# Sample keys turned in 32x32 blocks on VectorE and scored by 32-row matmuls, in a hybrid attention step on one Trainium2 core

## The reference

```python
z = rms_norm(x) @ w_in                        # q, k, v of branches A and B, gates
# A: 3 groups (window, dilation) = (128,1), (512,4), (2048,16), 8 heads of 64
idx = L + arange(t)[:, None] - arange(n + 1)[None, :] * dilation   # a query reads every d-th key
scores = einsum('bthd,btshd->bhts', q, k_ext[:, idx]) * d ** -0.5 - slope * steps * dilation
out_g = softmax(scores) @ v_ext[:, idx];  out_A = softmax(lse over groups) . out_g
# B: 4 heads, two maps over all 2048 + 8 keys (through page_table)
out_B = (softmax(q1 k1 - alibi) - lam * softmax(q2 k2 - alibi)) @ v
y = x + (sig(ma) * (silu(ga) * out_A @ w_a) + sig(mb) * (silu(gb) * rms(out_B) @ w_b)) @ w_out
```

## Time and profile before

| | us |
|---|---|
| median of 3 runs | 2002.45 (1999.88 to 2004.5) |
| the profiled execution | 2006.53 |
| its span | 2004.7 |
| TensorE busy | 1787.8 (89%) |
| VectorE, ScalarE, GpSimd busy | 623.6, 563.1, 620.6 |
| granted clock, mean | 0.953 |

### The profile page before, as it was taken

How to read it: one execution, slowest core, us unless ns; L and a number is a source line. 1 busy time by engine, 2 the same in 40 slices (tenths; PEclk the granted TensorE clock), 3 DMA queues, 4 the chain that set the end, 5 groups by cost and what they waited for, 6 DMA issues and landing times.

```text
span 2004.7 us, 31885 instructions
## 1 busy us (share of the span) xinstructions
PE 1787.8 (89%) x11560; PEld 1445.0 (72%) x11560; DVE 623.6 (31%) x1543; ACT 563.1 (28%) x1348; POOL 620.6 (31%) x763
## 2 busy tenths in 40 slices
PE   4899889999999999999957788777869999899899
PEld 3677556877799989999845565555647777677677
DVE  3321466221542217221533333333440104320321
ACT  3321356221442217220522222222211112211210
POOL 4663310466424644464500000000151215321210
PEclk8999999999999999999978889998889999899899
DMA  4136210434133441435169999999753754131542
GB/s 143 43 105 221 85 40 11 158 134 164 41 107 115 170 170 44 152 136 195 56 177 309 331 317 317 331 326 324 241 193 112 243 195 157 62 103 50 189 158 79
DMA packets 152794, 325.98 MB, mean 163 GB/s; under 512 B 24137, under 2 KB 45130, under 8 KB 151114
## 3 DMA queue, kind: packets, MB, share of 16 engines
q1 hardware_dynamic: 149130, 235.14, 36.1%
q10 hardware_dynamic: 3520, 88.90, 12.3%
HBM read 289.71 MB, written 121.57 MB: 205 GB/s over the span
## 4 chain that ended last, share of the span: by engine, by line
PE 68%; DMA 12%; issue 6%; POOL 5%; SPq 4%; DVE 3%; ACT 1%; ACTq 0%; DVEq 0%; POOLq 0%
PE ps L1573 15%; PE ps L1577 15%; PE ps L1574 15%; PE ps L1655 3%; PE ps L1606 3%; PE ps L1697 3%; PE ps L1675 3%; DMA v_in<-in_cache_a_kv 3%; DMA k_in<-in_cache_a_kv 2%; DMA raw<-in_w_in 2%; PE ps L1662 2%; DMA k_in<-in_cache_b_kv 2%; DMA v_in<-in_cache_b_kv 2%; POOL w_lo L719 1%; PE ps L1627 1%
## 5 line engine op out<-in xcount | busy, mean ns | idle before, releaser
L1573 PE MATMUL ps<-w_hi,hT_hi 128*128 128x512 f32 (+1 forms) x1440 | 591.1, 410 | 14.8 <-DVE w_lo L1137 6.5
L1577 PE MATMUL ps<-w_hi,hT_lo 128*128 128x512 f32 (+1 forms) x1440 | 579.3, 402 | 0.0
L1574 PE MATMUL ps<-w_lo,hT_hi 128*128 128x512 f32 (+1 forms) x1440 | 578.0, 401 | 0.0
L1573 PEld LDWEIGHTS ps<-w_hi,hT_hi 128*128 128x128 f32 (+1 forms) x1440 | 316.8, 220 | 71.8 <-issue 6.8
L1577 PEld LDWEIGHTS ps<-w_hi,hT_lo 128*128 128x128 f32 (+1 forms) x1440 | 316.5, 220 | 56.9 <-issue 0.4
L1574 PEld LDWEIGHTS ps<-w_lo,hT_hi 128*128 128x128 f32 (+1 forms) x1440 | 317.2, 220 | 53.5 <-issue 0.2
L719 POOL TENSOR_TENSOR w_lo<-raw,w_hi 128x512 fp32r<-128x512 f32 x160 | 210.0, 1315 | 433.6 <-ACT w_hi L884 433.3
L884 ACT ACTIVATE w_hi<-raw 128x512 fp32r<-128x512 f32 x176 | 110.3, 630 | 350.4 <-DMA raw<-in_w_in 302.9
L1697 PE MATMUL ps<-ident,k_in 128*128 128x128 f32 x928 | 140.0, 299 | 40.6 <-DMA k_in<-in_cache_b_kv 16.6
L1697 PEld LDWEIGHTS ps<-ident,k_in 128*128 128x128 f32 x928 | 112.3, 153 | 82.9 <-issue 44.0
L785 POOL TENSOR_SCALAR qz<-qT 64x128 f32<-64x128 f32 x208 | 109.2, 525 | 83.8 <-PE ps L1655 72.9
(11 more groups left out here) (159 smaller groups left out, 2063.3 us busy)
## 6 DMA issues: line engine op xcount, KB each, us to landing
out<-in_cache_a_kv ACTq DMA_DIRECT2D x32, 2040.0 KB, 8.4
raw<-in_w_in SPq DMA_DIRECT2D x144, 256.0 KB, 3.6
k_in<-in_cache_b_kv SPq DMA_DIRECT2D x128, 256.0 KB, 4.4
v_in<-in_cache_b_kv SPq DMA_DIRECT2D x128, 256.0 KB, 5.6
k_in<-in_cache_a_kv SPq DMA_DIRECT2D x104, 256.0 KB, 6.4
v_in<-in_cache_a_kv SPq DMA_DIRECT2D x104, 256.0 KB, 5.1
out<-in_cache_a_kv ACTq DMA_DIRECT2D x8, 2016.0 KB, 9.1
o_scr<-qT SPq DMA_DIRECT2D x16, 512.0 KB, 3.5
```

The source lines that it names most:

```text
L1573: pe.matmul(z, sh, w_hi[u % 2][:, k, :], start=(k == 0), stop=False)
L1574: pe.matmul(z, sh, w_lo[u % 2][:, k, :], start=False, stop=False)
L1577: ins = pe.matmul(z, sl, w_hi[u % 2][:, k, :], start=False, stop=(k == K - 1))
```

## The change

The key tiles are no longer turned by TensorE. VectorE transposes every 32x32 block of a tile in place, in `k_in`. After that, partitions 32i to 32i+31 hold, for each block of 32 keys, 32 of the head dimensions: a partition block i is a block of the tile's keys, and the columns `c * 128 + 32 * j` name the part j of the dimensions. A score is then a sum over four parts j, each a matmul over 32 rows; the four partition blocks i go to four PSUM banks and the four pairs c to four column blocks, so that a group of four tiles is 4 x 4 x 4 matmuls with 16 stationary columns and 128 streamed keys. GpSimd copies the queries to all four partition blocks (`q_rep`, rows now (c, half, query), 16 for each c).

The dilated tiles are scored against all eight queries; a table `bias_sa` holds 1e30 where a query does not read a key, as for the pages. So branch A's scores are 13 x 128 + 32 columns instead of 408. The groups are now 4, 4, 4, 1 tiles and four times four pages; key slots are 3 groups of four and are free once the group is scored; value slots are 12. Probabilities are transposed in nine pieces of up to four tiles through one bank (bank 4), copied by ScalarE to one of two buffers `pT`. The new keys and values are also stored in a DRAM scratch `new_scr` by sample and read back per sample. The minimum of branch B is taken over 4 partition-block strips with a table `ahead`, and its exponential is four instructions and one for the new keys.

```diff
+FIRST_S = (0, 4, 8, 12, 13, 17, 21, 25, 29)
+COLS_A = TILES_A * 32
+KEYS_A = TILES_A * P + NEW
...
-        NKS, NVS = 8, 16
+        NKS, NVS = 3, 12
+        k_in = place("k_in", [P, NKS, 4, CW], at=at)
...
+        def pieces_at(gg):
+            b, n = divmod(gg, 8)
+            if n >= 5:
+                return [(b, n - 5)]
+            return [(b - 1, p) for p in ((3,), (4,), (5,), (6,), (7, 8))[n]] if b else []
+        def keys_of(t, i, tiles):
+            return t[:, 0:tiles * P].rearrange("p (t f r) -> p t f r", f=4, r=32)[:, :, i, :]
...
-            for g in range(4):
-                sp.dma_start(v_in[0:NS, g, :], kept_new(g, 0)).then_inc(kn_in, 16)
...
-                    if kk >= NKS:
-                        sp.wait_ge(s_kt, kk - NKS + 1)
-                    sp.dma_start(k_in[:, kk % NKS, :], rows_s(kk, 0)).then_inc(sk_in[kk % NKS], 16)
+                    gg, j = key_slot(kk)
+                    b = kk // TILES_S
+                    if j == 0 and gg >= NKS:
+                        sp.wait_ge(s_qk, gg - NKS + 1)
+                    if kk % TILES_S == 0:
+                        if b:
+                            sp.wait_ge(s_qk, 8 * b - 4)
+                        sp.dma_start(k_new[:, :], new_rows(0, b)).then_inc(skn_in, 16)
+                    sp.dma_start(k_in[:, gg % NKS, j, :], rows_s(kk, 0)).then_inc(sk_in[gg % NKS][j], 16)
+                    if kk % TILES_S == TILES_S - 1:
+                        if b:
+                            sp.wait_ge(s_pu, 9 * b)
+                        sp.dma_start(v_new[:, :], new_rows(1, b)).then_inc(svn_in, 16)
                 vv = kk - V_LAG
                 if vv >= 0:
-                    if vv == 0:
-                        sp.wait_ge(s_nt, 1)
                     if vv >= NVS:
-                        sp.wait_ge(s_pv, vv - NVS + 1)
+                        sp.wait_ge(s_pu, piece_of(vv - NVS) + 1)
...
+            def queries(b, groups):
+                for i in range(4):
+                    for j in range(4):
+                        h = DEC_T * (j // 2)
+                        ins = pool.tensor_copy(q_rep[32 * i:32 * i + 32, groups, j, :, h:h + DEC_T],
+                                               qTs[32 * j:32 * j + 32, groups, :, b * DEC_T:(b + 1) * DEC_T])
+                return ins
...
+                for pb, p in pieces_at(gg) if gg < N_GROUPS + 5 else ():
+                    N = 9 * pb + p
+                    act.wait_ge(s_pt, N + 1)
+                    if N >= 2:
+                        act.wait_ge(s_pu, N - 1)
...
+                    else:
+                        act.activation(pT[:, N % 2, :, :], bank(4).rearrange("p (g q) -> p g q", g=4),
+                                       ACT.Copy).then_inc(s_pm, 1)
...
+                if n == 7:
+                    act.wait_ge(s_mb, b + 1)
+                    for i in range(4):
+                        part = keys_of(s_b, i, N_PAGES)
+                        act.activation(part, part, ACT.Exp, bias=stat[:, 18 + i:19 + i], scale=-1.0,
+                                       accum_out=stat[:, 22 + i:23 + i])
...
+                        uses = sum(len(group_tiles(g)) > j for g in range(gg % NKS, gg + 1, NKS))
+                        dve.wait_ge(sk_in[gg % NKS][j], 16 * uses)
+                        dve.transpose(k_in[:, gg % NKS, j, :], k_in[:, gg % NKS, j, :]).then_inc(s_kt, 1)
+                if b < DEC_B and n == 2:
+                    dve.wait_ge(skn_in, 16 * (b + 1))
+                    dve.transpose(k_new[:, :], k_new[:, :]).then_inc(s_ktn, 1)
+                if b < DEC_B and n == 3:
+                    dve.wait_ge(s_qk, gg + 1)
                     if b:
+                        dve.wait_ge(s_pt, 9 * b - 5)
+                    for i in range(4):
+                        biased_s(keys_of(s_a, i, TILES_A), by_tile(bank(i)[:, 0:COLS_A]), by_tile(bias_sa[:, i, :]),
+                                 stat[:, i:i + 1])
+                    biased_s(s_a[:, TILES_A * P:KEYS_A], bank(0)[:, COLS_A:COLS_A + NEW], bias_sn[:, 0, :],
+                             stat[:, 4:5])
+                    biased_s(s_bn[:, b % 2, :], bank(0)[:, COLS_A:COLS_A + NEW], bias_sn[:, 1, :],
+                             stat[:, 12:13]).then_inc(s_ta, 1)
+                    dve.wait_ge(s_ta, b + 1)
+                    dve.tensor_reduce(stat[:, 5:6], stat[:, 0:5], AX_X, ALU.min).then_inc(s_ma, 1)
+                if b < DEC_B and n == 5:
+                    dve.wait_ge(s_ea, b + 1)
+                    dve.reciprocal(stat[:, 7:8], stat[:, 6:7]).then_inc(s_rec, 1)
+                if b < DEC_B and n == 7:
+                    dve.wait_ge(s_qk, gg + 1)
+                    if b:
+                        dve.wait_ge(s_pt, 9 * b - 1)
+                    for i in range(4):
+                        ins = biased_s(keys_of(s_b, i, N_PAGES), by_tile(bank(i)), by_tile(bias_sb[:, :]),
+                                       stat[:, 8 + i:9 + i])
+                    ins.then_inc(s_tb, 1)
+                    dve.wait_ge(s_tb, b + 1)
+                    link(dve.tensor_tensor(stat[:, 13:17], stat[:, 8:12], ahead[:, :], ALU.subtract))
+                    link(dve.tensor_reduce(stat[:, 17:18], stat[:, 12:17], AX_X, ALU.min))
+                    dve.tensor_scalar(stat[:, 18:22], ahead[:, :], stat[:, 17:18], None, ALU.add).then_inc(s_mb, 1)
+                if b and n == 0:
+                    dve.wait_ge(s_pu, 9 * b - 5)
+                    dve.wait_ge(s_rec, 2 * b - 1)
+                    dve.scalar_tensor_tensor(out=om[:, 0, :], in0=bank(5)[:, 0:P], scalar=old[:, 7:8],
                                              in1=mask[:, :], op0=ALU.mult, op1=ALU.mult).then_inc(s_om, 1)
+                if b and n == 3:
                     dve.wait_ge(s_eb, b)
+                    link(dve.tensor_reduce(old[:, 27:28], old[:, 22:27], AX_X, ALU.add))
+                    link(dve.reciprocal(old[:, 28:29], old[:, 27:28]))
+                    dve.tensor_scalar(old[:, 29:30], old[:, 28:29], coef[:, 0:1], None, ALU.mult).then_inc(s_rec, 1)
                 if b and n == 4:
+                    dve.wait_ge(s_pu, 9 * b)
+                    dve.wait_ge(s_rec, 2 * b)
+                    dve.tensor_scalar(om[:, 1, :], bank(5)[:, 0:P], old[:, 29:30], None, ALU.mult).then_inc(s_om, 1)
...
-            def keys_turn(kk):
-                pe.wait_ge(sk_in[kk % NKS], 16 * (kk // NKS + 1))
-                if kk >= 3:
-                    pe.wait_ge(*copied_keys(kk - 3))
-                for c in range(NC):
-                    ins = pe.transpose(bank(kk % 3)[:, c * P:(c + 1) * P],
-                                       k_in[:, kk % NKS, c * P:(c + 1) * P], ident[:, :])
-                ins.then_inc(s_kt, 1)
...
+                T0, tiles = FIRST_S[n], FIRST_S[n + 1] - FIRST_S[n]
+                G = (2, 3, 3, 1, 0, 0, 0, 0)[n]
+                col = 32 * (T0 if n < 4 else T0 - TILES_A)
+                pe.wait_ge(s_kt, tiles_before(gg + 1))
                 if n == 0:
+                    pe.wait_ge(s_qa, b + 1)
                     if b:
+                        pe.wait_ge(s_tb, b)
+                if n == 4:
+                    pe.wait_ge(s_ta, b + 1)
+                if n == 3:
+                    pe.wait_ge(s_qb, b + 1)
+                for j in range(4):
                     for c in range(NC):
+                        for i in range(4):
+                            rows, d0 = slice(32 * i, 32 * i + 32), c * P + 32 * j
+                            ins = pe.matmul(bank(i)[quadrant(c), col:col + 32 * tiles], q_rep[rows, G, j, c, :],
+                                            k_in[rows, gg % NKS, 0:tiles, d0:d0 + 32],
+                                            start=(j == 0 and n in (0, 4)), stop=(j == 3), skip_group_check=True)
+                if n == 3:
+                    pe.wait_ge(s_ktn, b + 1)
+                    for j in range(4):
+                        for g in range(4):
+                            for c in range(NC):
+                                at_, d0 = COLS_A + g * DEC_T, c * P + 32 * j
+                                ins = pe.matmul(bank(0)[quadrant(c), at_:at_ + DEC_T],
+                                                q_rep[0:32, (g + 1) % 4, j, c, :],
+                                                k_new[:, d0 + g * DEC_T:d0 + (g + 1) * DEC_T], start=False,
+                                                stop=(j == 3), skip_group_check=True)
+                ins.then_inc(s_qk, 1)
...
+            def probs(b, p):
+                N = 9 * b + p
+                if p == 0:
+                    pe.wait_ge(s_ea, b + 1)
+                if p == 4:
+                    pe.wait_ge(s_eb, b + 1)
+                if N:
+                    pe.wait_ge(s_pm, N)
...
+            def values(b, p):
+                N = 9 * b + p
+                pe.wait_ge(s_pm, N + 1)
+                if p == 0 and b:
+                    pe.wait_ge(s_oc, 2 * b)
+                if p == 4:
```

(30 more changed lines are left out.)

413 lines of the change are left out of this document (102 added, 311 removed).

## The result

The changed kernel takes 2118.44 us, median of four runs (2111.82 to 2122.35), against 2003.47 for the kernel before on the same chip: a ratio of 1.0575 (95% interval 1.0547 to 1.0603). It is 115 us slower; 1987.5 had been forecast, and the range ended at 2052. The profiled execution took 2122.35 us with a span of 2120.6.

A forecast was written before the change was run, and what follows sets the result against it. The sample stage was taken as bound by load supply, with some loss to a late consumer. Head -10.6, seven periods of 46 against 48.1 us, and tail +11 gave about -15: 1987.5 us from 2002.45, range 1970 to 2052.

The forecast's parts named there:

- (c): Sample scores on TensorE: 128 instructions a group at 12.2 ns, 1.56 us; 14.0 us a sample, TensorE's work 25.6.
- forecast chain: Sample stage: TensorE's work 25.6 us plus exposed VectorE hand-overs 16.7, together 42.3 us a sample.
- R2: Rival, slower: sixteen blocks don't overlap in row direction, 4.0 us a group, 2093 us; at 25 ns about 2048; chance 0.14.
- (a): Key transposes leave TensorE: 0.12 us each, 13.8 us a sample; their copies out of PSUM go too.
- (b): VectorE transposes each key tile in place, 29 a sample plus new keys: 0.69 us each, 20 us a sample.
- R3: Rival, slower by VectorE: a block transpose takes 1.32 us, chain 52.3 us, time 2037 us; chance 0.07.
- (d): New hand-overs: four VectorE transpose groups a sample wait behind TensorE, 18.8 us, of which 16.7 exposed.
- (e): Load supply and slots: supply stays 42.4 us a sample; one round stepped through gives 45, taken as 46 with half-clock stretches.
- R1: Rival, no gain: period stays at 48 us through supply and coupling losses, head and tail cancel, 2002 us; chance 0.17.
- (f): Head of the sample stage: keys asked for earlier, new keys scored at 1041.5 against 1052.1 us, gain 10.6.
- (g): Tail, from the eighth sample's new keys to the first weight load: 43.6 us against 32.6, loss 11.
- R4: Rival, slightly slower: hand-overs cost twice, TensorE scores at half clock, period 49 to 50, 2010 to 2016 us; chance 0.12.

The follow-up runs named there:

- the run at 42 to 54 ns a record: Kernel before the change, plus 256 added short matmul records in each of three steps a sample, all on one array block: 2287.5 us (1.144).

## Why the prediction was wrong, by its steps

The step that failed is (c), the price of the scores, 14.0 us a sample, and with it TensorE's work of 25.6 us. It took a start-to-start time from a row of 32 instructions (12.2 ns) and multiplied it by 128, and had no term for instructions that aren't there yet. What the runs showed in its place is the period of 60.4 us as 38.0 busy, 13.9 of "issue" and 8.6 for VectorE, where the forecast chain had 25.6 and 16.7.

As a pace 12.2 ns was near: a group took 1.78 us at the high clock (1227.58 to 1229.36), 13.9 ns a record, against 1.56, and up to 2.64 us at the low one; R2's 4.0 us and its 25 ns floor didn't occur. What the row can't show is that 32 instructions sit inside one piece. A group of 128 records is exactly one piece. The 7008 added records are 876 a sample, 6.8 pieces, on top of some 4.3 (556 records: 116 transposes, 168 of scores, 248 of values, the rest probabilities and sums), so 11.2 pieces a sample. At the median of 4.84 us that is an estimate of 54 us, and 9 pieces for the scores are 44, not 14.0. The size of a piece was at hand: the page's q8 line against the count of records gives about 250 instructions a packet. Its time was not. In the kernel before 128 records last 10.4 us on average (x613 in 50 us), no gap marks the end of a piece, and no row has the time that the next one takes.

The Trainium skill, "Runtime: NRT & Kernel Launch", section on instruction fetch mechanics, has the pieces (16 KiB, 256 instructions, fetched by a queue of the engine's own) and says that fetching is hidden because the sequencer hands out instructions more slowly than they arrive. The size agrees with the 16.4 KB here. That the fetch is hidden agrees with the kernel before, at 10.4 us for 128 records, and with the run at 42 to 54 ns a record; at 10 to 14 ns a record it did not hold, with 3.62 us of gap in a piece. The measurement decides.

(a) was right in its size and worth nothing: the key transposes (13.8 us a sample) left TensorE, but it is as busy as before (38.0 us a period against 38.2), and the period was the supply's at 47.3 to 47.9 us in every version with few enough instructions. (b) was right: 678 ns against 0.69; R3 out. (d) named the right places and had too much: 8.6 us a period against 16.7 (82.9 over the stage, 17.4 of it one wait at its start); with the transposes shortened, gaps took most of their place, so part of a hand-over and part of a gap lie over each other.

(e) did not bind, so its 45 us was never reached in the changed kernel; the runs with half of the blocks and with wide groups show 47.3 and 47.5, so 46 was slightly low too. The 42.4 us of supply were reached by no run; the lowest period is 47.3 at a DMA share of 0.95. So with few enough instructions the change would have been R1's case, near no gain, and not the forecast's. (f) forecast 10.6 and got 8.2 from the start of the stage, with three gaps of 0.44, 1.87 and 3.49 us in it; as the stage began 14.6 us late, the new keys were scored 6.4 us later than before. (g) forecast a loss of 11 and got 23.5: the last scores end after 32.5 us, not 23.8 (1513.2), with gaps and low clock in them, and pieces of probabilities take 3.6 us each at a low clock (1523.34 to 1526.98), not 2.4.

R4 saw that TensorE would run at a lower clock, and it did (0.73 to 0.76). The run with half of the blocks had 0.70 and kept the loads' period, so the low clock alone isn't the loss; what the changed kernel would gain from the high clock no run shows.

Of the three signs of being wrong that the prediction named, none gave the cause: a group over 2.5 us (some took up to 2.64, most 1.8 to 2.4), a transpose over 1 us (0.678), over 20 us a sample of waiting for VectorE's keys (8.6). There was no sign for TensorE idle with nothing to wait for.

The sentence that nothing outside the stage moves by more than 1 us was wrong by 14.6 us. It gave the small writes ahead of each stage no price, and missed what is queued behind them: the table loads on SyncE and the padding of the queries on GpSimd. One run with them moved shows most of this.

## What to carry to other kernels

When a change trades few long matmuls for many short ones, count instructions as well as columns: for each 128 f32 matmul records (256 with their weight loads) allow about 5 us (here 3.8 to 6.3, with the DMA engines three quarters busy), and take at least the greater of this and the work; waits for other engines came partly on top. A row of 32 equal matmuls gives the pace inside a piece, never the pace of a thousand; and gaps marked "issue" inside a run of equal matmuls, at equal counts, are the sign to look for. Compare runs through the kernel before on the same chip: here those medians differed by 4 us, as much as some effects. Where the loads bound, work taken off TensorE was worth nothing, and a small transfer put ahead of others on an in-order queue cost some 10 us through what waits behind it.

## What the runs showed of the hardware that was not expected

- TensorE's instruction queue brought 16.4 KB a packet, one for 128 matmul records and their weight loads. Gap end to gap end was 4.84 us by the median at a DMA share of 0.77 (21 pairs, 3.8 to 6.3) and 4.2 at 0.47.
- f32 matmuls of 32 rows by 8 columns lay 42 to 54 ns apart on one array block (x256 in 10.76 to 13.82 us); when they went round four they lay some 9 ns apart (x185 in 1.71 us), and 15 ns behind a gap (x71 in 1.07 us from start to next start).
- VectorE's transposition of a 128x512 f32 tile in 32x32 blocks took 0.678 us, of 32x512 0.656, of 128x128 0.270, of 128x32 0.184: the time follows the columns, not the partitions.
